# Expert gate and up weights laid side by side, and a turned copy of x loaded first, in a two-layer trunk kernel on one core

## The reference, cut to what matters

```
for l in range(2):
    z = rms_norm(x, norm_mix[l]) @ w_in[l]              # 1024 x 3000
    x = x + concat(diff_attn(z), sparse_attn(z), mla(z)) @ w_out[l]   # 1024 x 1024
    h = rms_norm(x, norm_ffn[l])                        # router picks 2 of 32 experts
    for each expert e, its tokens t, its gates g:
        x[t] += g * ((silu(h[t] @ w_gate[l,e]) * (h[t] @ w_up[l,e])) @ w_down[l,e])
out = rms_norm(x, norm_final)
```

## Time and profile before

| what | us |
|---|---|
| median of 3 runs (1188.06 to 1188.47) | 1188.37 |
| span of the profiled execution, first to last instruction | 1185.7 |
| median less span | 2.7 |
| TensorE products busy | 921.0 (78% of the span) |
| ScalarE / VectorE busy | 195.9 / 333.8 |
| DMA, SP's queue (q1): 443.49 MB, share of 16 engines | 90.7% |
| DMA, ACT's queue (q10): 2.76 MB | 0.7% |
| mean rate of all DMA over the span | 378 GB/s |
| chain that ended last: DMA / TensorE | 60% / 35% |
| packets of all DMA (under 2 KB / under 8 KB) | 60504 (16368 / 33264) |

### The profile page before, as it was taken

The page is one execution under the profiler, slowest core; times in us unless marked ns, Lnnn a source line. Parts: engine busy times, 40 slices in busy tenths (PEclk is TensorE's granted clock), DMA queues, the critical chain, the costliest instruction groups (busy, mean ns, idle before and its releaser), DMA issues.

```text
span 1185.7 us, 23487 instructions
## 1 busy us (share of the span) xinstructions
PE 921.0 (78%) x10312; PEld 605.4 (51%) x10317; DVE 333.8 (28%) x974; ACT 195.9 (17%) x529; POOL 18.4 (2%) x37
## 2 busy tenths in 40 slices
PE   9999999766676676766799999997585847566765
PEld 5876566444444343434478766665253525334532
DVE  3555652211111111111147465521111111111112
ACT  2244331010100010101022442211010101000102
POOL 1000000000000000000010001000000000000000
PEclk9999999987888789888999999999787978798888
DMA  8976499999999999999998156999999999999994
GB/s 304 389 299 236 194 366 428 428 423 429 424 429 423 428 425 426 426 427 425 403 388 324 46 226 269 378 425 426 427 424 428 426 425 427 425 427 425 425 428 206
DMA packets 60504, 447.80 MB, mean 378 GB/s; under 512 B 10832, under 2 KB 16368, under 8 KB 33264
## 3 DMA queue, kind: packets, MB, share of 16 engines
q1 hardware_dynamic: 57664, 443.49, 90.7%
q10 hardware_dynamic: 2736, 2.76, 0.7%
HBM read 442.57 MB, written 3.67 MB: 376 GB/s over the span
## 4 chain that ended last, share of the span: by engine, by line
DMA 60%; PE 35%; issue 1%; DVE 1%; SPq 1%; ACT 1%; POOL 0%; POOLq 0%; ACTq 0%; DVEq 0%
DMA ring<-in_w_up 41%; DMA arena<-in_w_up 11%; PE pv L1818 9%; PE pj L1439 8%; DMA arena<-in_w_down 8%; PE pj L1445 2%; PE pj L1545 2%; PE pj L1676 2%; PE pj L1651 1%; PE pj L1685 1%; PE tr L1840 1%; PE lg L1469 1%; SPq L593 1%; PE tr L1479 1%; PE pj L1850 1%
## 5 line engine op out<-in xcount | busy, mean ns | idle before, releaser
L1818 PE MATMUL pv<-ring,xT 128*32 128x256 f32 x3136 | 293.0, 454 | 145.8 <-DMA ring<-in_w_up 92.7
L1818 PEld LDWEIGHTS pv<-ring,xT 128*32 128x32 f32 x3136 | 147.4, 126 | 241.3 <-issue 191.9
L1284 DVE TENSOR_SCALAR arena<-arena 128x128 f32<-128x128 f32 x64 | 14.5, 227 | 678.7 <-ACT arena L860 678.4
L1818 PE MATMUL pv<-arena,xT 128*32 128x256 f32 x640 | 89.2, 436 | 28.7 <-DMA ring<-in_w_up 28.7
L675 ACT ACTIVATE arena<-pv 128x256 f32<-128x256 f32 x64 | 24.6, 384 | 525.8 <-PE pv L1818 525.8
L1439 PE MATMUL pj<-xT,ring 128*128 128x256 f32 x448 | 100.3, 381 | 0.0
L1840 PE MATMUL tr<-ring,arena 128*32 128x256 f32 x1376 | 83.0, 379 | 15.1 <-issue 15.1
L1439 PEld LDWEIGHTS pj<-xT,ring 128*128 128x128 f32 x448 | 84.1, 190 | 13.3 <-issue 1.2
L1850 PE MATMUL pj<-arena 32*128 32x256 f32 x512 | 72.5, 399 | 8.1 <-ACT arena L675 8.1
L1850 PE MATMUL lg<-arena 32*128 32x256 f32 x512 | 72.5, 400 | 0.0
L1818 PEld LDWEIGHTS pv<-arena,xT 128*32 128x32 f32 x640 | 46.1, 121 | 47.5 <-issue 39.6
(11 more groups left out here) (244 smaller groups left out, 950.7 us busy)
## 6 DMA issues: line engine op xcount, KB each, us to landing
ring<-in_w_gate SPq DMA_DIRECT2D x46, 2048.0 KB, 44.6
ring<-in_w_up SPq DMA_DIRECT2D x46, 2048.0 KB, 38.9
ring<-in_w_down SPq DMA_DIRECT2D x42, 2048.0 KB, 42.9
arena<-in_w_down SPq DMA_DIRECT2D x14, 2048.0 KB, 45.1
arena<-in_w_gate SPq DMA_DIRECT2D x12, 2048.0 KB, 44.8
ring<-in_w_in SPq DMA_DIRECT2D x10, 2048.0 KB, 21.2
arena<-in_w_up SPq DMA_DIRECT2D x8, 2048.0 KB, 39.3
ring<-in_w_out SPq DMA_DIRECT2D x4, 2048.0 KB, 21.3
```

Of the source, the lines that this page charges most:

```text
L1818: ins = mm(gu_ps[i * CAP:(i + 1) * CAP, :], xg[:, j, c:c + CAP], w, start=(j == 0), stop=(j == KD - 1), tile_position=(0, i * CAP), skip_g ...
```

## The change

gate and up of an expert are laid side by side in DRAM (1024 columns for each of the 8 steps of a partition, 32 KB without a gap on each partition) and come in one transfer of 4096 KB into one of four places (`gu_place`); down weights go through three places of their own (`d_place`). `x` and `bias` now lie next to each other, so that the last of the places has no break. w_in's chunks and w_out's halves are laid out in DRAM as they lie in SBUF, so each partition's part is without a gap (up to 16 KB, before 2 KB for each step). The loads of a layer's first experts are written out by hand (`first_experts`). A copy of x turned by features, `x_turned`, is loaded first, half by half, into a part of the arena; in layer 0 VectorE reads it from there in place of PSUM, TensorE has no transposes, the products with the diagonals stand in the middle of the second half's products, and x itself comes behind the first chunk and the second turned half. GpSimd waits in layer 0 for VectorE to have read `x_turned` before it clears the pads that lie over it. Semaphores are renamed to match. The core of the diff:

```diff
+def loads_of(m):
+
+    order = [("gu", 0)]
+    for e in range(1, BODY - 1):
+        order += [("gu", e), ("d", e - 1)]
+    late = [("gu", BODY - 1), ("d", BODY - 2)] if m == ROUNDS - 1 else [("d", BODY - 2), ("gu", BODY - 1)]
+    return [(kind, m * BODY + e) for kind, e in order + late + [("d", BODY - 1)]]
+
+
+GU_PLACES, D_PLACES = 4, 3
+GU_LOADS = {1: 2, 2: 2}
+D_LOADS = {1: 2, 2: 2}
+SPLIT = GU_PLACES - 1
+REFILLED = GU_PLACES
...
+        x_turned = arena[:, 15 * SEQ + TOK * R5:][:, 0:TOK * D_MODEL].rearrange("p (t j s) -> p t j s", t=TOK, j=KD)
...
+        late_place = arena[:, ARENA - 2 * SLOT:]
+        flat_ring = ring.rearrange("p s n -> p (s n)")
+        gu_place = [flat_ring[:, 2 * i * SLOT:2 * (i + 1) * SLOT].rearrange("p (j n) -> p j n", j=KD) for i in range(3)]
+        gu_place.append(late_place.rearrange("p (j n) -> p j n", j=KD))
+        d_place = [flat.rearrange("p (k n) -> p k n", k=KE) for flat in (ring[:, 7, :], ring[:, 6, :], xb[:, 0:SLOT])]
...
         @block.sync
         def _(sp):
-            for s in range(ALL_SLOTS):
-                sp.sem_inc(slot_free[s], 1)
             n5, half = D_IN - IK, KD // 2
-            sp.dma_start(x[:, 0, :], x_tiled[0]).then_inc(x_in[0], 16)
+            def first_experts(l):
+                gu, down = gu_v[l * N_EXPERTS:], down_v[l * N_EXPERTS:]
+                if l < 1:
+                    sp.wait_ge(bias_ready, 1)
+                    sp.dma_start(bias_d[:, :], bias[:, 0:8, :].rearrange("p h k -> p (h k)")).then_inc(bias_out, 16)
+                sp.wait_ge(win_used[0], l + 1)
+                sp.wait_ge(win_used[1], l + 1)
+                sp.dma_start(gu_place[0], gu[0]).then_inc(gu_full[0], 16)
+                sp.wait_ge(win_used[2], l + 1)
+                sp.dma_start(gu_place[1][:, 0:half], gu[1][:, 0:half]).then_inc(gu_full[1], 16)
+                sp.wait_ge(index_used, at(l, 8, 8))
+                sp.dma_start(spare[1], down[SPLIT][:, 1]).then_inc(spare_full[1], 16)
+                sp.wait_ge(win_used[3], l + 1)
+                sp.dma_start(gu_place[1][:, half:], gu[1][:, half:]).then_inc(gu_full[1], 16)
+                if l == 0:
+                    sp.wait_ge(qk_ready, 1)
+                    load_small(sp, 1)
+                sp.wait_ge(win_used[4], l + 1)
+                sp.dma_start(gu_place[2][:, 0:half], gu[2][:, 0:half]).then_inc(gu_full[2], 16)
+                sp.wait_ge(lg_done, at(l, NS, 8))
+                sp.dma_start(gain_ffn, bcast_row(norm_ffn, l, D_MODEL)).then_inc(gain_f_in, 16)
+                if l == DEPTH - 1:
+                    sp.dma_start(gain_end, bass.AP(norm_final.tensor, norm_final.offset, [[0, P], [1, D_MODEL]])
+                                 ).then_inc(final_in, 16)
+                sp.wait_ge(win_used[5], l + 1)
+                sp.dma_start(gu_place[2][:, half:], gu[2][:, half:]).then_inc(gu_full[2], 16)
+                sp.wait_ge(pj_done, at(l, PJ_EV, PJ_EV))
+                sp.dma_start(spare[0], down[SPLIT][:, 0]).then_inc(spare_full[0], 16)
+                sp.wait_ge(ssq_ready, l * RMS + 5)
+                sp.dma_start(gu_place[3], gu[3]).then_inc(gu_full[3], 16)
+                if l < 1:
+                    sp.wait_ge(bias_out, 16)
+                sp.dma_start(d_place[2][:, KE // 2:], down[2][:, KE // 2:]).then_inc(d_full[2], 16)
+                sp.wait_ge(wout_used[1], l + 1)
+                sp.dma_start(d_place[0], down[0]).then_inc(d_full[0], 16)
+                sp.wait_ge(upper_spent, l + 1)
+                sp.dma_start(d_place[1][:, KE // 2:], down[1][:, KE // 2:]).then_inc(d_full[1], 16)
+                sp.wait_ge(wout_used[0], l + 1)
+                sp.dma_start(d_place[1][:, 0:KE // 2], down[1][:, 0:KE // 2]).then_inc(d_full[1], 16)
+                sp.wait_ge(sums_open, l + 1)
+                sp.wait_ge(x_weighted, at(l, TOK, TOK))
+                sp.dma_start(d_place[2][:, 0:KE // 2], down[2][:, 0:KE // 2]).then_inc(d_full[2], 16)
+                again = gu[REFILLED]
+                sp.wait_ge(steps_used, at(l, 2, 1))
+                sp.dma_start(gu_place[0][:, 0:2], again[:, 0:2]).then_inc(refill_in, 16)
+                sp.wait_ge(steps_used, at(l, 2, 2))
+                sp.dma_start(gu_place[0][:, 2:4], again[:, 2:4]).then_inc(refill_in, 16)
+                sp.wait_ge(gu_used[0], at(l, GU_FILLS, 1))
+                sp.dma_start(gu_place[0][:, 4:], again[:, 4:]).then_inc(gu_full[0], 16)
...
+            def turned(t):
+                sp.dma_start(x_turned[:, t].rearrange("p j s -> p (j s)"), x_turned_d[t]).then_inc(turned_in[t], 16)
+            turned(0)
             for i in range(2):
-                sp.dma_start(chunk(0, n5)[:, 2 * i:2 * i + 2, :], win_v[0][:, 2 * i:2 * i + 2, IK:D_IN]).then_inc(quarter_in[i], 16)
-            sp.dma_start(x[:, 1, :], x_tiled[1]).then_inc(x_in[1], 16)
+                sp.dma_start(chunk(0, n5)[:, 2 * i:2 * i + 2, :], win_v(0, 0)[:, 2 * i:2 * i + 2]).then_inc(quarter_in[i], 16)
             for l in range(DEPTH):
                 for i, (a, b) in enumerate(WIN_CHUNKS):
-                    s = slot_of(l, i)
-                    sp.wait_ge(slot_free[s], at(l, FILLS[s], 1))
+                    if l > 0:
+                        sp.wait_ge(gu_used[i // 2], l * GU_FILLS)
                     sp.sem_inc(passed["sp"], 1)
                     js = slice(half if l == 0 and i == 0 else 0, KD)
-                    sp.dma_start(chunk(s, b - a)[:, js, :], win_v[l][:, js, a:b]).then_inc(slot_full[s], 16)
+                    sp.dma_start(chunk(i, b - a)[:, js, :], win_v(l, i)[:, js]).then_inc(win_full[i], 16)
                     if l == 0 and i == 0:
+                        turned(1)
+                        for t in range(TOK):
+                            sp.dma_start(x[:, t, :], x_tiled[t]).then_inc(x_in[t], 16)
                         sp.dma_start(con[:, C_FIRST:], consts_d[:, C_FIRST:]).then_inc(more_consts_in, 16)
                     if l < 1 and i == 1:
                         load_small(sp, 0)
@@ -517,13 +542,12 @@
                     sp.wait_ge(lines_out, 16)
                 else:
                     sp.wait_ge(bias_out, 16)
-                    sp.wait_ge(slot_free[ALL_SLOTS - 1], at(l, FILLS[ALL_SLOTS - 1], 1))
+                    sp.wait_ge(d_used[2], l * D_FILLS[2])
                     sp.dma_start(bias[:, 0:8, :].rearrange("p h k -> p (h k)"), bias_d[:, :]).then_inc(bias_back, 16)
                 for i in range(2):
-                    s = slot_of(l, 6 + i)
-                    sp.wait_ge(slot_free[s], at(l, FILLS[s], 1))
-                    sp.dma_start(chunk(s, 512), wout_v[l][:, :, 512 * i:512 * i + 512]
-                                 ).then_inc(slot_full[s], 16)
+                    if l > 0:
+                        sp.wait_ge(d_used[1 - i], l * D_FILLS[1 - i])
+                    sp.dma_start(chunk(6 + i, 512), wout_v[l, i]).then_inc(wout_full[i], 16)
...
+                    if m == 0:
+                        first_experts(l)
+                    for kind, e in loads_of(m):
+                        if kind == "gu" and e > REFILLED:
+                            i = e % GU_PLACES
+                            sp.wait_ge(gu_used[i], at(l, GU_FILLS, gu_uses(e)))
+                            sp.dma_start(gu_place[i], gu_v[l * N_EXPERTS + e]).then_inc(gu_full[i], 16)
+                        elif kind == "d" and e >= SPLIT:
+                            i = e % D_PLACES
+                            sp.wait_ge(d_used[i], at(l, D_FILLS[i], d_uses(e)))
+                            ks = slice(len(spare) if e == SPLIT else 0, KE)
+                            sp.dma_start(d_place[i][:, ks], down_v[l * N_EXPERTS + e][:, ks]).then_inc(d_full[i], 16)
...
                 rms_of(own, base, 1, 0, 1, True)
                 rms_of(own, base, 2, 1, 2, True)
+                if l == 0:
+                    pool.wait_ge(xt_read, 2 * TOK)
                 for pad in (qpad, kpad):
                     own.mark(nc.gpsimd.memset(pad[:, :, :, C_NOPE + C_ROPE:64], 0.0))
...
-                        dve.wait_ge(xt_done, at(l, 4, 2 * t + half + 1))
-                        v.tensor_tensor(xT_raw[:, js, t * P:(t + 1) * P],
-                                        (tr, pv)[t][:, half].rearrange("p (j s) -> p j s", j=4),
+                        if l == 0:
+                            dve.wait_ge(turned_in[t], 16)
+                            src = x_turned[:, t, js]
+                        else:
+                            dve.wait_ge(xt_done, at(l - 1, 4, 2 * t + half + 1))
+                            src = (tr, pv)[t][:, half].rearrange("p (j s) -> p j s", j=4)
+                        v.tensor_tensor(xT_raw[:, js, t * P:(t + 1) * P], src,
                                         spread(gain_T[:, l, js], 2, P), ALU.mult).then_inc(xt_read, 1)
...
                 def turn_in(t):
-                    if l == 0:
-                        pe.wait_ge(x_in[t], 16)
-                    else:
```

(79 more changed lines are left out.)

222 lines of the change are left out of this document (59 added, 163 removed).

## The result

The changed kernel takes 1197.84 us (median of 4 runs, 1196.46 to 1201.28), the kernel before 1188.21 beside it (1187.81 to 1188.47): the ratio is 1.0087, 95% interval 1.0071 to 1.0102. It is 9.6 us slower; 1190.4 was forecast. The profiled execution took 1201.28, the slowest of the four, with a span of 1199.4, 13.7 more than the span before.

The account below looks back on a forecast made before the run. Attention was taken as bound by TensorE, then the expert stream by the DMA engines. +7.0 at the stream's start and -5.0 in it gave +2.0: span 1187.7, plus 2.7 to the median, 1190.4 us; range 1180 to 1198.

Parts of the forecast that it names:

- part 2: Layer 0's bias-line store, sharing engines packet by packet with w_in, starves; with clock and head's gain, +7.0 us at stream start.
- rival (a): Bias-line store not starved, engines sharing by bytes or cutting long packets; it lands at 37 to 39: 1182.1 us, chance 0.30.
- Part 1: Head of layer 0: without x's 16 transposes the first pair begins at 21.1 instead of 22.36, 1.3 us won.
- Rival (c): Head of layer 0 not shortened because x lands late; changes only the unstarved-store case, to 1183.4 us; counted within its 0.30.
- the wait passes at 46.6: ACT's wait in layer 0's head for the bias-line store ends at 46.6 us, leaving TensorE idle 6.3 us.
- the late case: In layer 0's head, small loads last as long as before, so the wait for the store passes 2.5 us later.
- The clock term: After TensorE's idling in layer 0's attention part its clock runs at half for a while: 2.0 us, bounds 0 and 2.9.
- Part 3: Expert stream of both layers: larger packets save 4.0 us and the eleventh place 1.0, so -5.0; the new load order costs nothing.
- its last transfer is again the down weights of expert 31: nothing: Expert stream: the new load order keeps the same bytes and the same last transfer, so it costs 0 us.
- rival (b): Store starved, but the expert stream no faster, 427 GB/s being the port's limit: +7.0, 1195.4 us, chance 0.20.
- The signs: Trace marks named beforehand: store wait, ACT and TensorE idling, clock, packet counts, stream slices at 428 to 431 GB/s, first pair.
- The other nothings: Effects put at 0 us: refill after expert 0 (1 to 2 lost if uncovered), wider w_out and layer 1's w_in packets.

Follow-up runs that it names:

- both repairs: The changed kernel with w_in in 2 KB packets and expert 29's down weights loaded ahead of expert 30's gate and up: 1179.55 us, ratio 0.9925.

## Why the prediction was wrong, by its own steps

**Right: what bounds, and the direction.** A microsecond before 163 us moves the whole stream: the first product of experts came 10.9 us later than before (172.91 against 161.98). The two kernels with the mended order, which differ in w_in's rows alone, show the rule without the loss at the end: with the large rows the first product comes 11.4 us later (171.63 against 160.26), layer 1 and the end of the span 10.7 (598.94 against 588.27, 1188.4 against 1177.7). The mechanism of part 2 happened as told, with turns of one to one between 16 KB and 1.5 KB, and rival (a), which shares by bytes, fell. The Trainium skill, page "DMA: Bandwidth & Descriptors", section on queues, rings and completion order, says that the engines take their queues in turn and drain a whole packet each time; 97 packets against 97 agree, with one row as one packet. The page gives 9 to 17 descriptors to a packet as typical; turns of that length do not show here, where the counts in single microseconds from 30 to 34 are 27 to 26, 23 to 24, 24 to 23 and 23 to 24.

**Part 1** gave 1.3 us and measured 1.7 at the first pair. The wait for the chunk's other half, put at 0.4, was 0.3 at most (24 products in 9.42 us, 9.13 in the kernel with w_in by 2 KB rows). The rms products waited for nothing: they start at 16.30 and the last half bank at 16.74, where 17.3 was forecast, as x's second half was there by 13.37 and not at 14.4. Rival (c) is out.

**Part 2, first miss: "the wait passes at 46.6".** It passed at 49.9. The round of one packet of each queue was right: 0.682 us predicted, 4 us over 97/16 packets, 0.66, measured. What failed is the begin and the count. The small loads were to end at about 21.5 us and q1 to have 25.5 packets an engine left when the store began, at 25.5. Up to 24 us q1 still moved little but small loads (568 packets, 0.25 MB in 20 to 24 us). The 80 packets of the store in 26 to 30 us, at 97 in 4, put its begin at 26.7, and until 46 us, when its large rows were nearly gone, q1 moved 7.18 MB more, 27 rows of 16 KB an engine (498 packets with the small ones, 31 an engine). This is the late case which that step named ("If the small loads last as long as before, 2.5 us later": 49.1) and did not take. TensorE then idled 10.19 us, where 6.3 was forecast; it came to the transposes of cn 8.7 us later than before (50.99 against 42.29), where 5.0 was forecast with 9 as the upper bound. The clock term was 2.0 and measured 2.2 in this trace, 1.6 in the kernel with the order mended. At the start of the stream this is 10.9 us where the sum had 7.0: 3.9 of the forecast's error.

**Part 3, second miss: the order of the loads, "its last transfer is again the down weights of expert 31: nothing".** The step failed because it went by the last transfer, and not by the order in which TensorE asks for the ones before it: TensorE stood 10.25 us for the down weights of expert 29. Mending it gave back 5.6 us. This step is the larger part of the error, and no rival had it. The two misses, 3.9 and 5.6, less the 1.3 that the stream brought beyond its term, make 8.2; the medians ask for 7.4. That 1197.84 lies inside the range of 1180 to 1198 is luck: its high end stood for rival (b) with the late small loads, and the stream did get faster.

**Part 3, the rate: -5.0.** Right in size. With both repairs the two expert parts take 428.1 and 435.4 us (first product of experts to the next layer or to the end), before 430.7 and 439.0: together 6.3 less in the profiled executions. Splitting the gate and up loads costs 4.7. The ceiling of 435 GB/s from the same page of the Trainium skill, from which the prediction estimated -12, was not reached: the sixteen windows have 428.8 in the mean and 431 at most. (Its 550 us at 427 GB/s would give -10 at 435, and -11 with the eleventh place. The line of part 2 also takes 426 GB/s for the window where the earlier trace rows has 424; through 426 its constant is 9.1 ns, through 424 it is 8.7, and no term moves by more than 0.3 us.) Rival (b), in which the stream doesn't speed up, fell as well.

**The signs.** Of those that part named, the wait at 45 to 50 us, equal packets, the clock of 0.50, a first pair near 21 and a stream at about 428 (slices of 423 to 436) came; the stands of ACT and TensorE were longer than the 8 to 10 and 6 to 7 given (13.14 and 10.19). None of them looked at the end of a layer.

**The other nothings.** After expert 0 the engines move 369 GB/s in 170 to 175 us of the kernel with both repairs, where TensorE starts the experts at 160.19, and 406 before, 161.91: a dent of 0.4 us, made up in the next five. The wider w_out and w_in of layer 1 left no wait in the chain, and attention in layer 1 takes 154.0 us (604.22 to 758.25) as before (592.64 to 746.67). Altogether, in medians: w_in's layout 12.7, the last round's order 5.6, and the rest of the change -8.7, together +9.6.

## What to carry to other kernels

Where two queues share the DMA engines by turns of packets, making the rows of one longer takes rate from the other: here rows eight times as long left the store 0.15 MB in 4 us instead of 0.70. Before widening a bulk transfer, look for a small one that somebody waits for at the same time, and hold the bulk back for it, or give it equal rows. When a list of loads is put in a new order, compare it with the order in which the engine uses them at the ends of the loop too, where hand-written exceptions stand.

## What the runs showed of the hardware

Turns between two queues stay one to one at a ratio of packet sizes of more than 10 (16 KB to 1.5 KB, 97 to 97 in 4 us, and 110 to 109 in the kernel before with w_in's layout alone); the smaller queue came down from 0.70 MB to 0.15 in that time. Loads of 4 MB with 32 KB packets ran at 428.8 GB/s, as two of 2 MB with 16 KB packets at 426.5; which of the two, packet or transfer, makes the difference is open. TensorE's clock fell with a stand of 2.48 us behind 35 products of zeros (36 in the program; 0.61 and 0.54 in the windows after) and held at 1.00 with one of 0.45.
